# Neighbourhood attention in a new order on TensorE, and latent scores head by head

## The reference

```
s_lat = q @ k_rows * scale + bias;  s_lat = where(col_mask, s_lat, -inf)
s_ctx = q @ k_ctx * scale
p = softmax(concat([s_lat, s_ctx]))
o = p[:, :512] @ v_rows + p[:, 512:] @ v_ctx
```

```
s = einsum('bqhd,bkhd->bhqk', q, k) * scale
p = softmax(s);  o = einsum('bhqk,bkhd->bqhd', p, v)
```

## Time and profile before

| | us |
|---|---|
| median of 3 runs (2271.65 to 2272.22) | 2272.01 |
| the profiled execution | 2271.57 |
| its span in the profile | 2269.8 |

### The profile page before, as it was taken

How to read it: one execution, slowest core, us unless ns; L and a number is a source line. 1 busy time by engine, 2 the same in 40 slices (tenths; PEclk the granted TensorE clock), 3 DMA queues, 4 the chain that set the end, 5 groups by cost and what they waited for, 6 DMA issues and landing times.

```text
span 2269.8 us, 32550 instructions
## 1 busy us (share of the span) xinstructions
PE 2202.0 (97%) x12322; PEld 1759.8 (78%) x12322; DVE 1219.8 (54%) x1873; ACT 1017.9 (45%) x1701; POOL 381.6 (17%) x249
## 2 busy tenths in 40 slices
PE   6999999989999999999999999999999999999998
PEld 3998776577778887877877788888888777888886
DVE  6640565564442206744565476664655755666645
ACT  5431557664365426643265433342432764333323
POOL 1332012000332430030002100014300021000243
PEclk9999999999999999999999999999999999999999
DMA  8122241103321222135401232223254012233331
GB/s 313 56 75 88 98 146 21 45 2 139 104 83 56 85 64 76 43 109 145 124 29 36 92 97 92 92 93 101 85 149 121 29 38 93 93 94 99 94 93 46
DMA packets 59151, 200.88 MB, mean 89 GB/s; under 512 B 8139, under 2 KB 8651, under 8 KB 58764
## 3 DMA queue, kind: packets, MB, share of 16 engines
q1 hardware_dynamic: 59020, 199.08, 27.5%
HBM read 187.19 MB, written 2.10 MB: 83 GB/s over the span
## 4 chain that ended last, share of the span: by engine, by line
PE 90%; ACT 4%; DVE 3%; issue 2%; DMA 0%; POOL 0%; SPq 0%; DVEq 0%; ACTq 0%; POOLq 0%
PE PS L935 7%; PE PS L933 7%; PE PS L934 7%; PE PS L2311 4%; PE PS L3101 4%; PE PS L3103 4%; PE PS L3102 4%; PE PS L2341 3%; PE PS L2327 3%; PE PS L1972 3%; PE PS L1126 2%; PE PS L1128 2%; PE PS L1127 2%; PE PS L1932 2%; PE PS L1268 2%; PE PS L1934 2%
## 5 line engine op out<-in xcount | busy, mean ns | idle before, releaser
L933 PE MATMUL PS<-H_HI,W_SPLIT 128*128 128x512 f32 x672 | 265.5, 395 | 0.0
L935 PE MATMUL PS<-H_HI,W_SPLIT 128*128 128x512 f32 x672 | 264.9, 394 | 0.0
L934 PE MATMUL PS<-H_LO,W_SPLIT 128*128 128x512 f32 x672 | 264.5, 394 | 0.0
L519 POOL TENSOR_TENSOR W_SPLIT<-WT,W_SPLIT 128x1024 fp32r<-128x1024 f32 x43 | 104.6, 2434 | 613.1 <-ACT W_SPLIT L508 495.5
L485 ACT ACTIVATE W_SPLIT<-WT 128x1024 fp32r<-128x1024 f32 x80 | 84.8, 1060 | 267.4 <-PE PS L935 267.4
L3451 DVE TENSOR_TENSOR W_SPLIT<-WT,W_SPLIT 128x1024 fp32r<-128x1024 f32 x80 | 98.0, 1225 | 150.1 <-ACT W_SPLIT L485 150.0
L1334 POOL TENSOR_TENSOR OUT_HALF<-WT,OUT_HALF 128x512 fp32r<-128x512 f32 x48 | 71.2, 1486 | 598.6 <-ACT OUT_HALF L1292 598.6
L3437 DVE TENSOR_TENSOR G_LO<-SB,G_HI 128x512 fp32r<-128x512 f32 x43 | 100.4, 2335 | 109.3 <-ACT G_HI L3250 109.3
L934 PEld LDWEIGHTS PS<-H_LO,W_SPLIT 128*128 128x128 f32 x672 | 126.0, 188 | 30.4 <-issue 0.5
L933 PEld LDWEIGHTS PS<-H_HI,W_SPLIT 128*128 128x128 f32 x672 | 126.2, 188 | 29.9 <-issue 0.5
L935 PEld LDWEIGHTS PS<-H_HI,W_SPLIT 128*128 128x128 f32 x672 | 126.2, 188 | 29.8
(11 more groups left out here) (424 smaller groups left out, 5571.3 us busy)
## 6 DMA issues: line engine op xcount, KB each, us to landing
WT<-weights SPq DMA_DIRECT2D x313, 512.0 KB, 3.6
SB<-SB SPq DMA_DIRECT2D x128, 64.0 KB
SB<-weights SPq DMA_DIRECT2D x13, 512.0 KB, 13.3
XT<-tokens SPq DMA_DIRECT2D x8, 768.0 KB, 5.9
SB<-rpb SPq DMA_DIRECT2D x8, 384.0 KB, 3.7
HT<-rpb SPq DMA_DIRECT2D x8, 384.0 KB, 4.1
out<-HT SPq DMA_DIRECT2D x4, 512.0 KB, 2.7
SB<-late SPq DMA_DIRECT2D x1, 1280.0 KB
```

Source lines behind the costliest of these rows:

```text
L519: g.tensor_tensor(w[:, 1, :], W[:, (g0 + t) % SLOTS, :], w[:, 0, :].bitcast(F32), ALU.subtract).then_inc(sem("w_lo"), 1)
L933: pe.matmul(PS[:, s, :], hi, H_HI[:, c, :], start=(c == 0), stop=False)
L934: pe.matmul(PS[:, s, :], hi, H_LO[:, c, :], start=False, stop=False)
L935: last = pe.matmul(PS[:, s, :], lo, H_HI[:, c, :], start=False, stop=(c == KC - 1))
```

## The change

Two methods are added, and the neighbourhood attention calls the first in place of pe. In it the transpositions of one of two steps come first, then the scores of the next two steps, then the other step's transpositions, and then the values of two steps one after the other. The second overrides scores for the latent attention: all parts of a head before the next head. VectorE's, ScalarE's and SyncE's programs are as they were.

```
+            def paired_pe(self, pe):
+
+                for a in range(self.scored_ahead - 4, self.S, 2):
+                    if a >= 0:
+                        self.turns(pe, a)
+                    for n in (a + 2, a + 3):
+                        if self.scored_ahead <= n < self.S:
+                            self.scores(pe, n)
+                    if 0 <= a + 1 < self.S:
+                        self.turns(pe, a + 1)
+                    for n in (a - 1, a):
+                        if n >= 0:
+                            self.values(pe, n)
+                            if n in self.final:
+                                self.spread(pe, self.final.index(n))
+                self.following.ahead_pe(pe)
...
+            def scores(self, pe, s):
+                u, t, lo, hi = self.steps[s]
+                pair, queries = self.units[u][0], slice(128 * t, 128 * t + 128)
+                for a in range(2):
+                    if s >= self.twice:
+                        pe.wait_ge(sem("at_exped"), self.b["exped"] + 2 * (s - self.twice) + a + 1)
+                    for at, b, e in self.key_parts(s):
+                        last = self.score(pe, PS[:, self.bank(s, a) + at // 512, at % 512:at % 512 + e - b], pair, a, queries, slice(b, e))
+                    last.then_inc(sem("at_scored"), 1)
...
-            att_od.pe(pe)
+            att_od.paired_pe(pe)
```

## The result

| | us |
|---|---|
| before, median of 4 | 2272.08 |
| changed, median of 4 (2287.69 to 2291.1) | 2287.99 |
| ratio, 95% interval | 1.0072 (1.006 to 1.0084) |
| profiled execution of the changed kernel, its span | 2287.79, 2286.0 |

The kernel became 16 us slower. The forecast was 2291.2 in a range of 2284 to 2303. The instructions are the same in number, 32550. In the rows of the changed kernel and the variants, the lines of VectorE and ScalarE in the attention stand some 17 lower in the file: L2477 is masked (L2460 before), L2487 VectorE's copy (L2470), L2429 the exponential (L2412), L2438 ScalarE's copy (L2421), L2508 the finish (L2491), and L2628 to L2630 the three products of a latent score (L2601 to L2603).

A forecast was written before the change was run, and what follows sets the result against it. TensorE's own sequence was taken to set the neighbourhood stage's time. Profiled 2271.57 + 17.6 (stage) - 1.1 (latent) + 2.7 (clock) = 2290.8, plus 0.4 for the median: 2291.2 us, range 2284 to 2303.

The forecast's parts named there:

- The chain: Neighbourhood attention: scores, two masked, VectorE's copy, transpositions take 3.21 us against 1.93 of work; about 1.2 us pause, 15 rounds.
- The second wait: Neighbourhood attention: copy of n-1 waits for values(n-3), transpositions(n) start at T + 2.91, just covered; 0.02 us per round.
- Rival B: Neighbourhood attention: the copy of n-1 behind late values binds too, 7 x 0.5 = 3.5 us more, 2294.8; 12%.
- Rival D: Neighbourhood attention: the new order shortens the chain by 0.3 us per round, 2286; 7%.
- The start: Start of neighbourhood stage: transpositions(0) at 863.13; transpositions(1) want 864.15 but need copy(0), so 866.42.
- The stage: Neighbourhood stage: laid out from transpositions(0) to the output projection, it ends 17.6 us later, the -2.7 included.
- The clock: Neighbourhood stage: 15 pauses bring 2 falls of TensorE's clock at 1.4 us, 2.7 us; bounds none and 25.
- rival C: Neighbourhood stage: the clock falls after most pauses, 12 x 1.7 = 20 us instead of 2.7, 2309; 11%.
- The latent part: Latent attention: scoring head by head removes head 1's wait for the exponential, -1.1 us; bounds 0 and 3.
- 3 x 0.26 + 3 x 0.12: Latent attention: the second head's score waits in three pairs, summed to the 1.1 us taken as saved.
- Rival A: Neighbourhood attention: no pause, copy early enough or TensorE fills it; only kind changes and latent waits saved, 2268.2; 5%.

The follow-up runs named there:

- order-only kernel: Changed kernel with only the neighbourhood attention's new TensorE order, latent scores as before; 2292.17 us, 1.0084 of before.
- values-between: Changed kernel, but values of step n-3 stand between the scores and the transpositions of n-1; 2275.24 us, 1.001 of before.
- old-order kernel: TensorE order of before, latent scores head by head, VectorE's copy ahead of masked in odd steps; 2270.03 us, 0.9981 of before.
- copy-first kernel: Changed kernel with VectorE's copy of step n-2 ahead of masked(n) in odd steps; 2268.56 us, 0.9986 of before.

## Why the prediction was right, and where a size was off

**The chain.** Forecast 1.17 + 0.62 + 0.62 + 0.80 = 3.21 from scores to transpositions. Measured 1.16 + 0.62 + 0.61 + 0.83 = 3.22. TensorE stood 16 times for this copy, where 15 were forecast: seven times 1.06 us, seven times 1.23, 2.23 at the start and 2.09 at the end. The one 0.32 us wait at the end of the stage before the change was this chain with its cover nearly gone, and its row gave the last term.

**The second wait.** Forecast: the copy behind the late values just covered, T + 2.91. Measured 885.25 - 882.28 = 2.97. From scores to scores it is 886.25 - 879.05 = 7.20 against 7.14, and with a spread 879.05 - 871.04 = 8.01 against 7.98. Rival B (0.5 us each) did not come. Rival D neither, the chain being no shorter than its rows.

**The start.** Transpositions(1) at 3.29 us after transpositions(0) in the forecast; 862.85 - 859.53 = 3.32 measured:

```profile
859.53 1.09 PE L2327 MATMUL PS<-SB 128*128 128x128 f32 x8
862.85 1.06 PE L2327 MATMUL PS<-SB 128*128 128x128 f32 x8 [2.23 <-DVE SB L2487]
```

**The stage.** Forecast +17.6, without the clock. Measured +19.83, of which 1.58 is a half-clock stretch after the stage's last pause (2.09 us), on the timeline of the changed kernel:

```profile
970.27 1.13 PE L2311 MATMUL PS<-SB 64*128 64x256 f32 x8
973.49 1.06 PE L2327 MATMUL PS<-SB 128*128 128x128 f32 x8 [2.09 <-DVE SB L2487]
974.49 3.62 PE L2341 MATMUL PS<-SB 128*64 128x128 f32 x32
978.04 1.09 PE L2327 MATMUL PS<-SB 128*128 128x128 f32 x8
```

From these transpositions to the next it is 978.04 - 973.49 = 4.55 us, and 2.97 elsewhere. The rest of the difference is 0.65: the fourteen intervals took 970.27 - 863.85 = 106.42 against 105.84, and 2.97 against 2.91 is one more such 0.06.

**The clock.** Forecast two falls at 1.4 in the stage; the profile has one, at 1.58. After the fourteen pauses of 1.06 and 1.23 us it did not fall once, so rival C did not come. Of the pauses of over 2 us some are followed by a fall and some not: in this profile the one of 2.23 at the start was not. The order-only kernel's profile has its one fall in this stage at 870.9, after the 2.23 us pause at the start, and there it cost only 0.55, since the scores that ran at half speed were followed by a shorter pause (timeline, order-only kernel; 3.77 us from scores to transpositions for 3.22):

```profile
870.43 3.60 PE L2311 MATMUL PS<-SB 64*128 64x256 f32 x32
874.20 1.10 PE L2327 MATMUL PS<-SB 128*128 128x128 f32 x8 [0.17 <-DVE SB L2487]
```

What the forecast did not count is that the stretch at 486 could go. It did. Its price can be read in the kernel before, from the second head's first product to the values of the same step, in pair 1 at full clock 457.69 - 453.85 = 3.84, in pair 2 across the stretch 491.00 - 485.81 = 5.19: 1.35 us. A stretch is not worth the same everywhere. The values-between and the old-order kernel have one from about 474.6 and 475.4. In the first, the two steps' values that it slows, up to their spread, take 479.82 - 474.09 = 5.73 us for 4.17 in the changed kernel, which has no stretch there; but behind the spread stands a wait for VectorE anyway, 0.87 us in the changed kernel. Their latent stages, 94.51 and 94.49 us, are only 0.7 longer than its 93.83.

```profile
457.69 0.66 PE L2341 MATMUL PS<-SB 128*64 128x128 f32 x8
...
491.00 0.66 PE L2341 MATMUL PS<-SB 128*64 128x128 f32 x8
```

**The latent part** is the term that was mis-sized: forecast -1.1, measured -3.8. About 1.4 is the clock, which comes and goes from execution to execution. The waits are worth 2.2 to 2.4, not 1.1. The step that failed is "3 x 0.26 + 3 x 0.12": I took the printed idle time for the loss. Products of 256 columns that follow each other stand 0.12 apart; the one that waited came at 453.85, 0.54 after its predecessor at 453.31, so 0.42 was lost there, and from it to the next (454.07) it is 0.22 instead of 0.12. The printed 0.26 is what remains between two modelled ends. In the changed kernel (timeline, latent scores) the second head's first product, at 454.25, follows without loss:

```profile
453.57 0.39 PE L2628 MATMUL PS<-QK_HI 96*128 96x512 f32 x1
...
454.03 0.39 PE L2630 MATMUL PS<-QK_HI,QH_LO 96*128 96x512 f32 x1
454.25 0.28 PE L2628 MATMUL PS<-QK_HI 96*128 96x256 f32 x1
454.37 0.28 PE L2629 MATMUL PS<-KH_LO,QK_HI 96*128 96x256 f32 x1
```

So a wide step that waited gains 0.53, and one that waited without a printed idle gains 0.21: 0.74 a pair, three pairs, 2.2. Whole steps say the same: from the values ahead of its scores to the transpositions behind them, the first such step of pair 1 took 455.69 - 451.27 = 4.42 us before and 455.30 - 451.41 = 3.89 after. That the maximum of head 0 can start sooner brought nothing, as forecast.

**Rival A** needed the copy to let the transpositions start 1.93 us after the scores, or TensorE to fill the pause. Neither came in the changed kernel. The work to fill it with was there: values(n-3), which the values-between kernel runs in this place without a wait, began behind the waiting transpositions in every round, so TensorE kept the order of its program. The prediction says that no row of before could tell this. One could: at 453.85 the second head's scores wait, and the first head's other part stood behind them and began at 454.31, timeline of before:

```profile
454.31 0.39 PE L2601 MATMUL PS<-QK_HI 96*128 96x512 f32 x1
```

It waits for nothing but what the first head's scores at 452.97 had waited for, and in the changed kernel it comes right behind them, at 453.57 after 453.11 (row above). With VectorE's queue turned round the copy is in time, and the price named for A, 2268.2, is what the copy-first kernel took, 2268.56; that is luck, for the split is another: less from the order, more from the latent part. That VectorE was idle for a quarter of the stage said nothing about this copy.

**The sum.** Forecast +17.6 for the stage, +2.7 for its clock and -1.1 for the latent part, 19.2; measured 18.25 + 1.58 - 3.75 = 16.1.

**Does the latent part make falls of the clock rarer?** The latent stage has one and three of them in the two profiles with the old scores, and none in six and one in two of the eight with the new. The mean granted clock that is recorded for every execution says more. On the first chip it is at most 0.996 in all 27 executions of before, and 0.997 in five of the 11 with only the latent part changed; the means of these rounded values are 0.99544 and 0.99600. So the clock is halved less often with it. The difference, 0.00056, is 1.3 us of 2270; this estimate and the 2.2 for the waits make 3.5, near the 3.7 between the medians. What stays open is why the clock falls after one wait and not after another of the same length.

## What to carry to other kernels

Before moving work on the engine that sets the time, take each wait of the moved pieces and walk up the other engine's queue: what stands ahead of the instruction waited for, and does that wait for something that the move has pushed later? A saving of 0.17 us on a change of kind cost 1.2 us, since it took the cover off a queue of three instructions; turning two entries of that queue round gave it back. And read a loss from the distance of starts, not from the idle time printed between modelled ends.

## What the runs showed of the hardware that was not expected

The printed idle before a product can understate what a wait costs: 0.26 us printed, 0.53 us of time. Before the long pauses it was near the whole: 1.23 printed, 1.29 from starts (3.22 against 1.93).

A half-clock stretch of TensorE is not a matter of the kernel alone. The order-only kernel's latent stage, with the instructions of before, had three (clock 0.50 for 3.42, 3.41 and 3.41 us) where before's profile had one. Much of the spread of executions goes with them: those of before on the first chip take 2271.7 us on average where the recorded mean clock is 0.996, 2273.1 at 0.995 and 2274.4 at 0.994.

A stretch of 3.4 us at half clock cost 1.58 us where TensorE's own work followed it, and 0.55 to 0.7 where a wait for another engine took up the rest.
